# ScalarE drains the latent queries and keys in the second mixer kind, and the latent rotations move behind VectorE's first low parts

## The reference, cut to what matters

```python
def token_mixer(u, w_in, b_gate, ...):
    z = u @ w_in
    qa, ka, va, cq, ckv, kr, gl = jnp.split(z, SPLIT_POINTS, axis=-1)
    qa = apply_axial_rope(rmsnorm(qa, q_norm_g), cos_a, sin_a)      # grouped queries, 8 heads of 64
    ka = apply_axial_rope(rmsnorm(ka, k_norm_g), cos_a, sin_a)      # grouped keys, 2 heads
    ya = blocked_attention(qa, ka, va, 1.0 / math.sqrt(GQA_HEAD_DIM))
    qb = (rmsnorm(cq, q_a_norm_g) @ w_q_up).reshape(b, s, MLA_HEADS, MLA_QK_DIM)
    q_nope, q_rope = qb[..., :MLA_NOPE_DIM], qb[..., MLA_NOPE_DIM:]
    q_rope = apply_axial_rope(q_rope, cos_b, sin_b)                 # latent rotation
    kvb = (rmsnorm(ckv, kv_a_norm_g) @ w_kv_up).reshape(b, s, MLA_HEADS, MLA_NOPE_DIM + MLA_V_DIM)
    k_nope, vb = kvb[..., :MLA_NOPE_DIM], kvb[..., MLA_NOPE_DIM:]
    k_rope = apply_axial_rope(kr, cos_b, sin_b)
    ...
    yb = blocked_attention(qb, kb, vb, 1.0 / math.sqrt(MLA_QK_DIM))
    ...
```

## Time and profile before

| | us |
|---|---|
| median of three executions | 3443.34 |
| lowest, highest | 3441.73, 3443.44 |
| the profiled execution, its own time | 3441.55 |
| its span from first to last instruction | 3439.7 |
| TensorE busy in it | 3400.9 |
| ScalarE busy | 1530.3 |
| VectorE busy | 2087.8 |
| first such mixer, scores start at | 2074.02 |
| second such mixer, scores start at | 2804.65 |

### The profile page before, as it was taken

The page is one execution under the profiler, slowest core; times in us unless marked ns, Lnnn a source line. Parts: engine busy times, 40 slices in busy tenths (PEclk is TensorE's granted clock), DMA queues, the critical chain, the costliest instruction groups (busy, mean ns, idle before and its releaser), DMA issues. The chain is left out here.

```text
span 3439.7 us, 46281 instructions
## 1 busy us (share of the span) xinstructions
PE 3400.9 (99%) x17572; PEld 2761.2 (80%) x17572; DVE 2087.8 (61%) x2990; ACT 1530.3 (44%) x2388; POOL 1989.7 (58%) x2338
## 2 busy tenths in 40 slices
PE   9999999999999999999999999999999999999999
PEld 8888868888888888748888887788788876888887
DVE  5556666655764468766645667326767575238667
ACT  4334454333533355675333537434444555335444
POOL 6555645555655658745665557554655665546564
PEclk9999999999999999999999999999999999999999
DMA  4223203233222322202332220123222210232321
GB/s 173 89 77 117 85 20 118 79 110 111 86 98 91 130 70 93 71 1 83 123 111 103 83 76 26 56 92 123 98 98 92 86 59 8 93 105 92 114 107 62
DMA packets 87726, 301.56 MB, mean 88 GB/s; under 512 B 9936, under 2 KB 14544, under 8 KB 87120
## 3 DMA queue, kind: packets, MB, share of 16 engines
q1 hardware_dynamic: 85392, 296.50, 24.4%
q10 hardware_dynamic: 2112, 2.10, 0.2%
HBM read 296.46 MB, written 2.10 MB: 87 GB/s over the span
## 5 line engine op out<-in xcount | busy, mean ns | idle before, releaser
L408 POOL TENSOR_TENSOR w_lo<-w_raw,w_hi 128x256 fp32r<-128x256 f32 x1754 | 1364.6, 812 | 1091.5 <-ACT w_hi L381 841.9
L419 PE MATMUL bank<-xh,w_hi 128*128 128x512 f32 x2544 | 997.8, 392 | 3.9 <-issue 1.5
L421 PE MATMUL bank<-xh,w_lo 128*128 128x512 f32 x2544 | 989.2, 389 | 0.0
L420 PE MATMUL bank<-xl,w_hi 128*128 128x512 f32 x2544 | 989.2, 389 | 0.0
L381 ACT ACTIVATE w_hi<-w_raw 128x1024 fp32r<-128x1024 f32 (+2 forms) x485 | 498.5, 1039 | 671.3 <-DMA w_raw<-in_ffn_up 269.3
L419 PEld LDWEIGHTS bank<-xh,w_hi 128*128 128x128 f32 x2544 | 478.1, 188 | 106.5 <-issue 4.6
L420 PEld LDWEIGHTS bank<-xl,w_hi 128*128 128x128 f32 x2544 | 478.2, 188 | 99.7 <-issue 2.4
L421 PEld LDWEIGHTS bank<-xh,w_lo 128*128 128x128 f32 x2544 | 478.0, 188 | 99.5
L408 POOL TENSOR_TENSOR extra_lo<-extra_raw,w_hi 128x256 fp32r<-128x256 f32 x264 | 229.8, 905 | 126.1 <-ACT w_hi L381 113.1
L1099 DVE TENSOR_TENSOR y_tok<-y_tok,bank 128x512 f32<-128x512 f32 x232 | 157.4, 685 | 223.1 <-PE bank L978 223.1
L1133 DVE TENSOR_TENSOR work<-bank,sqsum 128x512 f32<-128x512 f32 x88 | 60.7, 690 | 267.7 <-PE bank L421 267.7
(11 more groups left out here) (454 smaller groups left out, 6154.2 us busy)
## 6 DMA issues: line engine op xcount, KB each, us to landing
w_raw<-in_ffn_up SPq DMA_DIRECT2D x176, 512.0 KB, 3.5
w_raw<-in_b_ffn_up SPq DMA_DIRECT2D x64, 512.0 KB, 3.5
extra_raw<-in_ffn_down SPq DMA_DIRECT2D x52, 512.0 KB, 4.5
w_raw<-in_b_gates SPq DMA_DIRECT2D x48, 512.0 KB, 3.4
extra_raw<-in_b_ffn_down SPq DMA_DIRECT2D x40, 512.0 KB, 4.5
w_raw<-in_od_in SPq DMA_DIRECT2D x33, 512.0 KB, 3.5
w_raw<-in_b_in SPq DMA_DIRECT2D x24, 512.0 KB, 3.6
w_raw<-in_ffn_down SPq DMA_DIRECT2D x20, 512.0 KB, 3.4
```

The lines of the kernel that those rows point to most:

```text
L408: ins = pool.tensor_tensor(lo_of(g, part), raw_of(g, part), hi_of(g, part).bitcast(F32), ALU.subtract)
L419: pe.matmul(out, wh, hi, start=first, stop=False)
L420: pe.matmul(out, wh, lo, start=False, stop=False)
L421: return pe.matmul(out, wl, hi, start=False, stop=last)
```

## The change

`upn` and `kn` tiles are drained by ScalarE with a copy, in the order of the list, each copy waiting until all tiles before it are drained. In the list the four `upn` tiles follow each other, and `rotup` 0 and 1 stand between `kn` 1 and `kn` 2. VectorE makes the first two low parts at `kn` 0 and `kn` 1 as before, which is ahead of the rotations now. The three later roundings of grouped queries move behind the last drain and behind the loading of the exponential's table. TensorE's wait for the rotations moves from the start of the attention to the first `joint` products.

```diff
@@ attend_pe
                     pe.wait_ge(probs_ready, g)
+                    pe.wait_ge(rotated, c.at("rotated") + len(ROTS2))
                     for q, (query, key) in enumerate(u["joint"]):
@@ ORDER2
-        ORDER2 += [("upr", 0), ("rot", 3), ("upr", 1), ("turn", 0), ("upn", 0), ("rotup", 0), ("upn", 1), ("rotup", 1)]
-        ORDER2 += [("upn", 2), ("upn", 3)] + [("kn", i) for i in range(4)]
+        ORDER2 += [("upr", 0), ("rot", 3), ("upr", 1), ("turn", 0)] + [("upn", i) for i in range(4)]
+        ORDER2 += [("kn", 0), ("kn", 1), ("rotup", 0), ("rotup", 1), ("kn", 2), ("kn", 3)]
@@ mix2_pe
             pe.wait_ge(acc_drained, drained(c.tiles + len(TILES2) - 1))
-            pe.wait_ge(rotated, c.at("rotated") + len(ROTS2))
@@ mix2_act
-                if (kind, i) == ("kn", 1):
-                    act.wait_ge(rotated, c.at("rotated") + len(ROTS2))
-                    for q in (1, 2, 3):
-                        round_grouped(act, q)
                 if (kind, i) in LINS2 or (kind in ("upr", "upn") and UPS2.index((kind, i)) % 2 == 0) or (kind, i) == ("kn", 0):
                     round_ahead(act, g + (1 if g < c.blocks + OPEN else 0))
                     g += 1
+                if kind in ("upn", "kn"):
...
+                    act.wait_ge(acc_drained, drained(T + n - 1))
+                    act.activation((b_qn if kind == "upn" else b_kn)[:, i, :], bank[(T + n) % ACCS][:], ACT.Copy)\
+                       .then_inc(acc_drained, 1)
...
             act.activation(red[:, 0, 11:12], meancol[:, 0:1], ACT.Exp)
+            act.wait_ge(acc_drained, drained(T + len(TILES2) - 1))
+            act.wait_ge(rotated, c.at("rotated") + len(ROTS2))
+            for q in (1, 2, 3):
+                round_grouped(act, q)
@@ mix2_dve
-                elif kind in ("upr", "upn"):
...
+                elif kind == "upr":
...
                 elif kind == "kn":
...
-                    dve.tensor_copy(b_kn[:, i, :], src[:]).then_inc(acc_drained, 1)
                     if i < 2:
                         j = (4, 0)[i]
                         dve.wait_ge(grouped_rounded, SPLITS * L + i + 1)
```

More of the change, by code:

```diff
@@ L2410, in mix2_act @@
                     g += 1
+                if kind in ("upn", "kn"):
+                    u = UPS2.index((kind, i)) if kind == "upn" else 0
+                    if kind == "kn" and i == 3:
+                        act.wait_ge(blocks_done, block_done(c.blocks + len(LINS2) + 3))
+                    elif kind == "kn":
+                        act.wait_ge(up_done, 6 * c.at("tables") + 3 + i + 1)
+                    elif u % 2:
+                        act.wait_ge(blocks_done, block_done(c.blocks + len(LINS2) + u // 2))
+                    else:
+                        act.wait_ge(up_done, 6 * c.at("tables") + u // 2 + 1)
+                    act.wait_ge(acc_drained, drained(T + n - 1))
+                    act.activation((b_qn if kind == "upn" else b_kn)[:, i, :], bank[(T + n) % ACCS][:], ACT.Copy)\
+                       .then_inc(acc_drained, 1)
                 if kind in ("qk", "cq", "kv"):
@@ L2548, in mix2_dve @@
                     dve.tensor_tensor(dst, dst, work[:, 0, :], ALU.add).then_inc(rotated, 1)
-                elif kind in ("upr", "upn"):
-                    u = UPS2.index((kind, i))
-                    if u % 2:
-                        dve.wait_ge(blocks_done, block_done(B + len(LINS2) + u // 2))
-                    else:
-                        dve.wait_ge(up_done, 6 * L + u // 2 + 1)
-                    dve.tensor_copy(b_qr[:, i, :] if kind == "upr" else b_qn[:, i, :], src[:]).then_inc(acc_drained, 1)
+                elif kind == "upr":
+                    if i:
+                        dve.wait_ge(blocks_done, block_done(B + len(LINS2)))
+                    else:
+                        dve.wait_ge(up_done, 6 * L + 1)
+                    dve.tensor_copy(b_qr[:, i, :], src[:]).then_inc(acc_drained, 1)
                 elif kind == "kn":
[L2557 to L2560, removed]
-                    dve.tensor_copy(b_kn[:, i, :], src[:]).then_inc(acc_drained, 1)
                     if i < 2:
```

## The result

The changed kernel takes 3453.86 us (median of 8 executions, 3451.58 to 3455.78), the kernel before 3442.55 (8 executions, 3440.05 to 3443.83): the ratio is 1.0035 with a 95% interval of 1.0026 to 1.0044, so it is 11.3 us slower. The forecast was 3453.5. Of all executions that this document counts one was slow (11879.81 us, in experiment 7), and its ratio leaves it out.

What follows compares the result with a forecast made beforehand. TensorE bounds the kernel, working 3400.9 of 3439.7 us. A stall of 8.2 us plus a clock term of 2.8 gives 11.0, added to 3442.5: 3453.5 us, range 3449.5 to 3457.5.

Steps and rivals of the forecast that it cites:

- The place and the wait: First scores in both mixers: TensorE waits 4 to 5 us each for a ScalarE key copy, standing still 4.8 us.
- The lag of the load: Gates block ahead of the first key copy: its rounding starts 3.55 us after the last query projection ends, 3.65 in mixer two.
- One sign of being wrong: ScalarE in the first mixer: the prediction is wrong if it copies the first keys before 2070.
- The chain: From gates rounding through key copies, grouped rounding, low parts and rotations to the scores: 4.05 and 4.15 us later per mixer.
- bound upward: Both low parts and the rotation's sum slowed beside GpSimd's work: about 1.0 us more per mixer.
- stall term: Later start of the first scores, summed over both mixers: 8.2 us.
- The bound downward: The gates block's load lands 0.6 us sooner, as no other block is in flight: 0.6 us less per mixer.
- Rival 2: Key copies: ScalarE isn't held by the gates block, so not slower, about −0.2 us, 3442.3 us; chance 0.06.
- The clock: Behind the pause before the scores, TensorE runs at the lower clock: 1.4 us per mixer, 2.8 in all.
- rival 4: Clock stays low for two stretches at both places: 8.2 + 6.6 = 14.8 us, 3457.3 us; chance 0.08.
- Rival 1: Same stall before the scores, but the clock stays at its upper level: 8.4 us, 3450.9 us; chance 0.20.
- Late exponentials: First unit's exponential, behind ScalarE's table load and three roundings: costs TensorE 0.1 us per mixer, vanishing behind the slow clock.

Runs made afterwards that it cites:

- experiment 7: Kernel before, with one of the four latent value tiles computed between the last key matmul and the first scores; 3441.28 us, ratio 0.9995.
- experiment 2: Changed kernel with ScalarE rounding the gates block behind the two grouped roundings, not ahead of the first key copy; 3449.54 us, ratio 1.0020.
- 8: Kernel of experiment 2 with the first two grouped roundings at the second query tile and VectorE's rotations waiting for the second key copy; 3444.51 us, ratio 1.0009.
- experiment 3: Kernel before with the change's list order and its move of the three later roundings, all drains left on VectorE; 3454.09 us, ratio 1.0033.
- experiment 4: Changed kernel, drains on ScalarE, with the list order of before and VectorE waiting there for ScalarE's copy; 3444.05 us, ratio 1.0004.
- experiment 5: Kernel of experiment 4, gates block rounded only ahead of the last key copy, three later grouped roundings back at the second key tile; 3441.57 us, ratio 0.9998.
- experiment 6: Changed kernel with 22 dense 128x512 matmuls into a free bank ahead of TensorE's wait for the last drain; 3451.35 us, ratio 1.0027.
- experiment 10: Changed kernel timed again without a new edit, on one chip with the dense-filler kernel; 3455.72 us, ratio 1.0039.

## Why the prediction was right

- **The place and the wait.** As forecast, the scores' wait for a ScalarE copy, twice. The pause was put at 4.8 us and is 5.4. The lag of the load holds to the digit: the last query projection ends at 2063.84 + 0.39, the rounding starts 3.55 later. One sign of being wrong came up by the letter, ScalarE copies the first keys before 2070 (2068.74). It was given as a time of the trace of before, and this execution is 1.8 us ahead; the copy starts 4.51 us behind the end of the projection, where 4.52 was worked out. VectorE stood still for 13.34 us, where some ten were expected.
- **The chain.** From the rounding to the scores 8.44 us were worked out and 9.09 measured (2067.78 to 2076.87). The link that was mis-sized is the pair of low parts, 0.94 + 0.60 against 2.09 (2070.56 to 2072.65). Both run beside GpSimd's low parts of the gates block, where the sum had one of them so; this was half of the bound upward. So the stall term is 9.3 us for 8.2. The rows show how the two engines meet:

```profile
2070.30 0.74 POOL L408 TENSOR_TENSOR w_lo<-w_raw,w_hi 128x256 fp32r<-128x256 f32 x1
2070.56 1.03 DVE L2572 TENSOR_TENSOR qk_lo<-b_qk,hi_a 128x512 fp32r<-128x512 f32 x1 [13.34 <-ACT hi_a L2387]
2071.00 1.17 POOL L408 TENSOR_TENSOR w_lo<-w_raw,w_hi 128x256 fp32r<-128x256 f32 x1
2071.51 1.21 DVE L2572 TENSOR_TENSOR qk_lo<-b_qk,hi_a 128x512 fp32r<-128x512 f32 x1
```

VectorE's subtractions end 0.55 us behind the end of the GpSimd instruction in which they started (2071.04 to 2071.59, 2072.17 to 2072.72), and GpSimd's second instruction ends 0.58 behind VectorE's first. The two engines look as if they took turns. Of the twenty sums and subtractions of two such tiles at L2561 and L2572 in this profile, the ten that started within a GpSimd instruction ended 0.55 us behind it, and the ten others took 0.69.

- **The bound downward.** It was to come from a load that lands 0.6 us sooner because no other is under way. No run shows that: in the trace of before this load of the first mixer is already the only one under way, and from issue to landing it takes 3.5 us before and after.
- **Why it stalls.** The two halves stand by experiments 2 and 8, the order as the cause by 3 against 4, ScalarE's copy as good as VectorE's by 5. Rival 2 (ScalarE isn't held) is wrong for the change; its picture holds for the kernel of experiment 5, where nothing is ahead of the copies.
- **The clock.** It fell in both mixers. The term was 2.8 us for 4.3 in the profiled execution. It was sized by one low stretch of 3.3 us per mixer, with two to three us of it behind the scores' start. The low level lasted 6.8 us at either place, 5.9 and 3.7 of them behind the scores' start. So the condition of rival 4, two stretches at both places, was met, and its price of 6.6 us was not, since 0.9 and 3.1 us passed while TensorE stood still. Rival 1 (the clock holds) put the change 8.4 us above the kernel before; the dense filler, which makes it so, is 9.4 above it in experiment 6. The rule of the Trainium skill, "TensorE: Matmul & The Clock Gate", section "What's actually happening", that idleness is followed by the slower clock, agrees with the four pauses over 5 us in the two profiles of the change, the two of 5.53 and 5.57 in experiment 3 and both of 2.87 us in experiment 2.
- **Late exponentials.** Put at 0.1 per mixer and nothing behind a slow clock. In the change TensorE doesn't wait for them, so nothing is right; with the clock up it is 0.6 (experiment 6), so the 0.1 was too small. The link was also another: the 0.1 came from ScalarE's three roundings, but ScalarE is done with them 0.43 us before the first exponential and waits for the row maximum, which ends late beside GpSimd's low part.
- **The sum.** The two terms were each too small, 11.0 for 13.6 in the rows. That the time came out 0.4 us from the forecast is in part luck. The profiled spans are 10.1 apart, the medians 11.3, and when the same kernel was timed again, in experiment 10, it was 13.2 us above the kernel before. Low stretches at other places, which the forecast left out, differ from one execution to the next: the last 20 us left aside, there are three in the profile of before, none in the one after and four in that of experiment 10. How much of these a pause takes the place of was not settled.

## What to carry to other kernels

Before a drain is moved to a less busy engine, look at what that engine has queued ahead of it: a copy behind an instruction that waits for a DMA is as late as the DMA, however idle the engine is by its share. A step that has slack where it stands (here the rounding of grouped parts, ten us early) loses it when it is written behind the moved work. Work of another engine that moves along with it (here GpSimd's low parts) can land beside an instruction on the path. And a pause on the engine that bounds the kernel is to be priced with what its clock does next.

## What was not expected of the hardware

Sixteen 128x128 float32 matmuls, which kept TensorE busy by the records for 3.7 us, were followed in one mixer of two by the lower clock after a pause of 1.9 us; 22 matmuls of 128x512 with 0.4 to 0.6 us of pause left the clock at 1.00 in all four mixers of two profiles. The pauses of 2.87 us in both mixers of experiment 2 were followed by the lower clock, those of up to 1.7 us in experiment 4 were not. And a VectorE sum or subtraction of two SBUF tiles of 128x512 that started within a GpSimd instruction ended 0.55 us behind it, ten times of ten at two lines of the profile after (1.03 to 1.21 us in all, where one alone takes 0.69); one of 128x2 ended 0.02 behind (1.18 us, where it took 0.28 before). No run moved GpSimd's work alone to test this.
